# A decoder layer on one core: meta rows folded to 128 partitions, input tiles turned ahead in six PSUM banks, first weight chunk split before them

## The reference

```python
def rmsnorm(x, g):
    xf = x.astype(jnp.float32)
    y = xf * lax.rsqrt(jnp.mean(xf * xf, axis=-1, keepdims=True) + EPS)
    return (y * g.astype(jnp.float32)).astype(x.dtype)
...
    h = jnp.concatenate([meta, x], axis=1)     # (1, 16 + 256, 2048)
    u = rmsnorm(h, pre_mix_g[i])
    proj = u @ w_in[i]                         # 2048 x 4608
    q, k, v, u_pool, u_conv = jnp.split(proj, splits, axis=-1)
    # three head groups, joined and normed, @ w_out, residual
    # u = rmsnorm(h, pre_ffn_g); (silu(u @ w_gate) * (u @ w_up)) @ w_down, residual
```

## Time and profile before

| | us |
|---|---|
| median of 3 runs (lowest, highest) | 1124.66 (1122.86, 1125.36) |
| profiled execution, its own time | 1124.34 |
| its span, first to last instruction | 1122.5 |
| PE busy | 1105.9 |
| DVE busy | 697.9 |
| ACT busy | 528.7 |
| POOL busy | 21.8 |

### The profile page before, as it was taken

How to read it: one execution, slowest core, us unless ns; L and a number is a source line. 1 busy time by engine, 2 the same in 40 slices (tenths; PEclk the granted TensorE clock), 3 DMA queues, 4 the chain that set the end, 5 groups by cost and what they waited for, 6 DMA issues and landing times.

```text
span 1122.5 us, 17667 instructions
## 1 busy us (share of the span) xinstructions
PE 1105.9 (99%) x6544; PEld 979.7 (87%) x6544; DVE 697.9 (62%) x812; ACT 528.7 (47%) x635; POOL 21.8 (2%) x39
## 2 busy tenths in 40 slices
PE   9999999999999999999999999999999999999997
PEld 8999999999888888888888888888888888888885
DVE  5599885646646866666666666666666545444444
ACT  6544444646554564444444444444444434343442
POOL 2000101101000000000000000000000000000000
PEclk9999999999999999999999999999999999999999
DMA  7665534444376366656665666566656555555553
GB/s 245 190 185 168 171 102 125 150 139 135 121 295 211 118 211 213 189 170 201 190 187 177 198 188 189 182 193 191 191 179 195 190 190 197 195 189 197 189 194 111
DMA packets 165998, 203.53 MB, mean 181 GB/s; under 512 B 6304, under 2 KB 133600, under 8 KB 165168
## 3 DMA queue, kind: packets, MB, share of 16 engines
q1 hardware_dynamic: 164800, 197.30, 55.8%
q10 hardware_dynamic: 576, 4.19, 1.0%
q0 software_dynamic: 576, 1.40, 0.4%
HBM read 200.77 MB, written 2.10 MB: 181 GB/s over the span
## 4 chain that ended last, share of the span: by engine, by line
PE 93%; DVE 3%; ACT 2%; DMA 1%; issue 0%; SPq 0%; DVEq 0%; ACTq 0%
PE ps L1065 28%; PE ps L1067 15%; PE ps L1398 7%; PE ps L1397 7%; PE ps L1399 7%; PE ps L1050 5%; PE ps L1052 5%; PE ps L1053 5%; PE ps L1305 3%; PE ps L1307 3%; PE ps L1306 3%; DVE w_lo L724 1%; DMA arena<-in_pre_mix_g 1%; PE ps L1163 1%; PE ps L1249 1%; PE ps L1197 1%
## 5 line engine op out<-in xcount | busy, mean ns | idle before, releaser
L724 DVE TENSOR_TENSOR w_lo<-raw,w_hi 128x1024 fp32r<-128x1024 f32 x368 | 449.4, 1230 | 351.1 <-ACT w_hi L425 350.8
L425 ACT ACTIVATE w_hi<-raw 128x1024 fp32r<-128x1024 f32 x368 | 388.3, 1059 | 474.3 <-PE ps L1067 252.3
L1065 PE MATMUL ps<-u,w_hi 128*128 128x512 f32 x1408 | 491.2, 392 | 1.7 <-DVE u L819 0.8
L1067 PE MATMUL ps<-u,w_lo 128*128 128x256 f32 x1408 | 394.9, 280 | 0.0
L1065 PEld LDWEIGHTS ps<-u,w_hi 128*128 128x128 f32 x1408 | 264.1, 188 | 61.4 <-DVE w_lo L724 1.1
L1067 PEld LDWEIGHTS ps<-u,w_lo 128*128 128x128 f32 x1408 | 265.3, 188 | 0.0
L1050 PE MATMUL ps<-u,w_hi 128*128 128x272 f32 (+1 forms) x576 | 168.9, 293 | 0.0
L1052 PE MATMUL ps<-u,w_hi 128*128 128x272 f32 (+1 forms) x576 | 165.8, 288 | 0.0
L1053 PE MATMUL ps<-u,w_lo 128*128 128x272 f32 (+1 forms) x576 | 165.6, 287 | 0.0
L1399 PE MATMUL ps<-w_hi,ffn 128*128 128x512 f32 x352 | 136.9, 389 | 0.0
L1398 PE MATMUL ps<-w_lo,ffn 128*128 128x512 f32 x352 | 136.9, 389 | 0.0
(11 more groups left out here) (174 smaller groups left out, 625.5 us busy)
## 6 DMA issues: line engine op xcount, KB each, us to landing
raw<-in_w_gate SPq DMA_DIRECT2D x88, 512.0 KB, 4.5
raw<-in_w_up SPq DMA_DIRECT2D x88, 512.0 KB, 4.4
raw<-in_w_down SPq DMA_DIRECT2D x88, 512.0 KB, 4.1
raw<-in_w_in SPq DMA_DIRECT2D x72, 512.0 KB, 3.6
raw<-in_w_out SPq DMA_DIRECT2D x32, 512.0 KB, 4.4
arena<-in_x SPq DMA_DIRECT2D x2, 1024.0 KB, 6.2
arena<-in_x ACTq DMA_DIRECT2D x2, 1024.0 KB, 8.8
out<-f_acc SPq DMA_DIRECT2D x3, 512.0 KB, 2.7
```

What stands on the lines that cost most here:

```text
L425: act.activation(w_hi[:, slot, :], raw[:, slot, :], ACT.Copy).then_inc(hi_done, 1)
L724: dve.tensor_tensor(w_lo[:, slot, :], raw[:, slot, :], hi_view(w_hi[:, slot, :]), ALU.subtract).then_inc(lo_done, 1)
L1065: pe.matmul(ps[:, bank + m, :].rearrange("p (a t) -> p a t", a=2), w_hi[:, slot, at], u[:, kt, :, 0:SEQ], start=first and k == 0, stop=Fal ...
L1067: mm = pe.matmul(ps[:, bank + m, 0:SEQ], w_lo[:, slot, at], u[:, kt, 0, 0:SEQ], start=False, stop=last and k == len(kts) - 1, skip_group_c ...
```

## The change

Meta: its 16 rows of 2048 are loaded as 128 partitions of 256 (partition 8t + s holds eighth s of row t). ACT squares them 256 wide; PE adds the eight partial sums of a row with a matrix of ones in blocks of eight (`blk`, made by POOL with a memset and two selects); ACT scales; PE turns them in two transposes; ACT copies the result (`xmt`), and POOL multiplies by the gain, rounds and subtracts into `u[:, :, :, 0:META]`, before it issues the side weights' DMAs, for which it now also waits for x tile 1. x tiles: DVE squares the first and ACT the second half of each, in the order of their landing; scaled copies come as halves of tile 0 and quarters of tile 1. PE turns them (256 columns per kt) into banks 2 to 7, two kt to a bank (`x_turned`), eighteen transposes before the first product and the others after chunks 0, 1 and 2. The first projection waits for `u_lo` tile by tile (`first_proj`). ACT and DVE split chunk 0 before input tile 0, chunk 1 after tile 5, chunk 2 after tile 9, chunk 3 after tile 13. The gain row is loaded from ACT's queue. The parameter vectors are turned before chunk 4. Fillers: 9, 5 and 19.

```diff
-WARM_LOAD, WARM_ROWS, WARM_PARTS, WARM_FFN = 26, 10, 4, 23
+WARM_LOAD, WARM_SUM, WARM_ROWS, WARM_FFN = 9, 5, 19, 23
...
-    VEC_AT, TURN_AT = 3, 4
+    VEC_AT = CK
+    HALF, QUART = D // 2, D // 4
+    MSEG = P // META
+    XBANKS = 6
...
-            sp_eng.dma_start(xr[0:META, 2, :], meta).then_inc(x_landed[2], 16)
+            sp_eng.dma_start(xr[:, 2, 0:D // MSEG], meta.rearrange("t (s c) -> (t s) c", s=MSEG)).then_inc(x_landed[2], 16)
             for m in range(NQ):
                 sp_eng.dma_start(xr[:, m, :], x[0, m * P:(m + 1) * P, :]).then_inc(x_landed[m], 16)
-            sp_eng.dma_start(grow[0:KT, :], pre_mix_g.rearrange("a (c p) -> (a c) p", p=P)).then_inc(grow_landed, 16)
...
+            pool.memset(blk, 1.0).then_inc(blk_step, 1)
             pool.wait_ge(const_step, 6)
+            pool.wait_ge(blk_step, 1)
+            blk3 = blk.rearrange("p (t s) -> p t s", s=MSEG)
+            pool.affine_select(blk3, blk3, [[-MSEG, META], [0, MSEG]], ALU.is_ge, 0.0, base=0,
+                               channel_multiplier=1).then_inc(blk_step, 1)
+            pool.wait_ge(blk_step, 2)
+            pool.affine_select(blk3, blk3, [[MSEG, META], [0, MSEG]], ALU.is_ge, 0.0, base=MSEG - 1,
+                               channel_multiplier=-1).then_inc(blk_step, 1)
...
+            pool.wait_ge(meta_kept, 1)
+            pool.wait_ge(grow_done, 1)
+            gains = vec[:, V_PRE:V_PRE + KT].rearrange("p (k a) -> p k a", a=1).to_broadcast([P, KT, META])
+            pool.tensor_tensor(xmg, xmt, gains, ALU.mult).then_inc(meta_done, 1)
+            pool.wait_ge(meta_done, 1)
+            pool.tensor_copy(u[:, :, 0, 0:META], xmg).then_inc(meta_done, 1)
+            pool.wait_ge(meta_done, 2)
+            pool.tensor_tensor(u[:, :, 1, 0:META], xmg, u[:, :, 0, 0:META].bitcast(F32), ALU.subtract).then_inc(meta_done, 1)
+            pool.wait_ge(x_landed[1], 16)
             pool.dma_start(wpl, w_pool.rearrange("a g c d -> c (a g) d")).then_inc(sw_landed, 16)
...
+        def x_turned(kt, lo=0, hi=SEQ):
+            at = kt // XBANKS % 2 * SEQ
+            return ps[:, 2 + kt % XBANKS, at + lo:at + hi]
...
+            act.dma_start(grow[0:KT, :], pre_mix_g.rearrange("a (c p) -> (a c) p", p=P)).then_inc(grow_landed, 16)
             act.preload_act_table_set("natural_log_exp_and_others")
             act.wait_ge(const_step, 6)
             act.wait_ge(x_landed[2], 16)
-            act.activation(xsm[0:META], xr[0:META, 2, :], ACT.Square, accum_out=ss0[0:META, 2:3]).then_inc(ss_act, 1)
-            act.wait_ge(ss_act, 1)
-            inv_rms(r0[0:META, 2:3], ss0[0:META, 2:3], D, r0_done)
+            act.activation(xsm, xr[:, 2, 0:D // MSEG], ACT.Square, accum_out=ss0[:, 2:3]).then_inc(ss_act, 1)
+            act.wait_ge(ssm_made, 1)
+            inv_rms(r0[:, 2:3], ps[:, 3, 0:1], D, r0_done)
             act.wait_ge(r0_done, 1)
-            act.activation(xsm[0:META], xr[0:META, 2, :], ACT.Copy, scale=r0[0:META, 2:3]).then_inc(xs_act, 1)
-            act.wait_ge(x_landed[1], 16)
-            act.activation(xs[:, 1, 0:D // 2], xr[:, 1, 0:D // 2], ACT.Square, accum_out=ss0[:, 1:2]).then_inc(ss_act, 1)
-            act.wait_ge(ss_dve, 3)
-            inv_rms(r0[:, 0:2], ss0[:, 0:2], D, r0_done)
-            act.wait_ge(r0_done, 2)
-            act.activation(xs[:, 1, 0:D // 2], xr[:, 1, 0:D // 2], ACT.Copy, scale=r0[:, 1:2]).then_inc(xs_act, 1)
+            act.activation(xsm, xr[:, 2, 0:D // MSEG], ACT.Copy, scale=r0[:, 2:3]).then_inc(xs_act, 1)
             act.wait_ge(grow_turned, 1)
             act.copy(vec[:, 0:KT], ps[:, 0, 0:KT]).then_inc(grow_done, 1)
+            act.wait_ge(meta_turned, 1)
+            act.copy(xmt.rearrange("p (s h) t -> p s h t", h=2),
+                     ps[:, 0, SEQ:2 * SEQ].rearrange("p (h t s) -> p s h t", h=2, s=MSEG)).then_inc(meta_kept, 1)
+            for m in range(NQ):
+                act.wait_ge(x_landed[m], 16)
+                act.activation(xs[:, m, HALF:D], xr[:, m, HALF:D], ACT.Square, accum_out=ssx[:, m, 1:2]).then_inc(ss_act, 1)
+                act.wait_ge(ss_dve, 2 * m + 2)
+                inv_rms(r0[:, m:m + 1], ss0[:, m:m + 1], D, r0_done)
+            def scaled(m, n):
+                cols = slice(n * QUART, (n + 1) * QUART)
+                act.activation(xs[:, m, cols], xr[:, m, cols], ACT.Copy, scale=r0[:, m:m + 1]).then_inc(xs_act, 1)
+            def input_tiles(kts):
+                for kt in kts:
+                    act.wait_ge(u_made, kt + 1)
+                    act.activation(u[:, kt, 0, META:TOK], x_turned(kt), ACT.Copy,
+                                   scale=vec[:, V_PRE + kt:V_PRE + kt + 1]).then_inc(u_hi, 1)
+            split(0)
+            act.wait_ge(r0_done, 3)
+            scaled(1, 1)
             act.wait_ge(grow_done, 1)
-            for kt in range(KT):
-                act.wait_ge(u_made, kt + 1)
-                act.activation(u[:, kt, 0, :], ps[:, 4 + kt % 4, 0:TOK], ACT.Copy,
-                               scale=vec[:, V_PRE + kt:V_PRE + kt + 1]).then_inc(u_hi, 1)
-                if kt % CK == CK - 1:
-                    split(kt // CK)
+            input_tiles(range(0, 6))
+            split(1)
+            input_tiles(range(6, 10))
+            split(2)
+            scaled(1, 3)
+            input_tiles(range(10, 14))
+            split(3)
+            input_tiles(range(14, 16))
...
+            for m in range(NQ):
+                dve.wait_ge(x_landed[m], 16)
+                dve.scalar_tensor_tensor(xs[:, m, 0:HALF], xr[:, m, 0:HALF], 1.0, xr[:, m, 0:HALF], ALU.mult, ALU.mult,
+                                         accum_out=ssx[:, m, 0:1]).then_inc(ss_dve, 1)
+                dve.wait_ge(ss_dve, 2 * m + 1)
+                dve.wait_ge(ss_act, m + 2)
+                dve.tensor_tensor(ss0[:, m:m + 1], ssx[:, m, 0:1], ssx[:, m, 1:2], ALU.add).then_inc(ss_dve, 1)
+            def scaled(m, lo, hi):
+                dve.tensor_scalar(xs[:, m, lo:hi], xr[:, m, lo:hi], r0[:, m:m + 1], None, ALU.mult).then_inc(xs_dve, 1)
+            def input_tiles(kts):
+                for kt in kts:
+                    dve.wait_ge(u_hi, kt + 1)
+                    dve.scalar_tensor_tensor(u[:, kt, 1, META:TOK], x_turned(kt), vec[:, V_PRE + kt:V_PRE + kt + 1],
+                                             hi_view(u[:, kt, 0, META:TOK]), ALU.mult, ALU.subtract).then_inc(u_lo, 1)
             dve.wait_ge(r0_done, 2)
+            scaled(0, 0, HALF)
+            dve.wait_ge(r0_done, 3)
+            scaled(1, 0, QUART)
+            scaled(0, HALF, D)
+            split(0)
+            input_tiles(range(0, 2))
+            scaled(1, HALF, 3 * QUART)
+            input_tiles(range(2, 6))
+            split(1)
+            input_tiles(range(6, 10))
+            split(2)
+            input_tiles(range(10, 14))
+            split(3)
+            input_tiles(range(14, 16))
...
+            pe.wait_ge(blk_step, 3)
+            pe.wait_ge(ss_act, 1)
+            pe.matmul(ps[:, 3, 0:1], blk, ss0[:, 2:3], start=True, stop=True).then_inc(ssm_made, 1)
+            keep_warm(WARM_SUM)
             pe.wait_ge(const_ready, 1)
             pe.wait_ge(grow_landed, 16)
             pe.transpose(ps[:, 0, 0:KT], grow[0:KT, :], ident[0:KT, 0:KT]).then_inc(grow_turned, 1)
+            pe.wait_ge(xs_act, 1)
+            pe.wait_ge(grow_done, 1)
+            for h in range(2):
+                mm = pe.transpose(ps[:, 0, SEQ + h * P:SEQ + (h + 1) * P], xsm[:, h * P:(h + 1) * P], ident)
+            mm.then_inc(meta_turned, 1)
             keep_warm(WARM_ROWS)
+            def turn_rows(m, kts):
                 for kt in kts:
+                    if m == 0:
+                        pe.wait_ge(xs_dve, 1 if kt < KT // 2 else 3)
+                        if kt >= 2 * XBANKS:
+                            pe.wait_ge(u_lo, kt - XBANKS + 1)
+                    else:
+                        if kt < CK:
+                            pe.wait_ge(xs_dve, 2)
+                        elif kt < KT // 2:
+                            pe.wait_ge(xs_act, 2)
+                        elif kt < 3 * CK:
+                            pe.wait_ge(xs_dve, 4)
+                        else:
+                            pe.wait_ge(xs_act, 3)
+                        if kt >= XBANKS:
+                            pe.wait_ge(u_lo, kt - XBANKS + 1)
+                    mm = pe.transpose(x_turned(kt, m * P, (m + 1) * P), xs[:, m, kt * P:(kt + 1) * P], ident)
+                    if m == 1:
+                        mm.then_inc(u_made, 1)
+            pe.wait_ge(r0_done, 1)
+            turn_rows(0, range(0, 8))
+            turn_rows(1, range(0, 2))
+            turn_rows(0, range(8, 12))
+            turn_rows(1, range(2, 6))
+            pe.wait_ge(meta_kept, 1)
+            pe.wait_ge(meta_done, 3)
+            LATER = {0: [(1, range(6, 10))], 1: [(1, range(10, 12)), (0, range(12, 14)), (1, range(12, 14))],
+                     2: [(0, range(14, 16)), (1, range(14, 16))]}
...
```

(17 more changed lines are left out.)

47 lines of the change are left out of this document (10 added, 37 removed).

## The result

The changed kernel takes 1118.19 us (median of 5 runs, 1117.63 to 1118.53) beside 1124.66 (1122.86 to 1126.67); the ratio is 0.9941, 95% interval 0.9927 to 0.9956: 6.5 us faster (5.0 to 8.2 by the interval), where 5.1 were forecast.

The account below looks back on a forecast made before the run. TensorE, busy 99% of the span, was taken as the bound. Gain 5.1 us: 3.55 before the first product, 4.06 of turns replaced by 1.54, less 1.0 new waiting; 1124.66 - 5.1 = 1119.56, rounded 1119.5, range 1117.0 to 1122.4.

Parts of the forecast that it names:

- The sum: Whole kernel: fifth chunk starts at 30.0 instead of 35.10 us, so the time falls by 5.1 us.
- The block: Everything after the fifth chunk's start moves as one: what the fifth chunk gains, the end gains.
- the late fall: Granted clock drops in mid kernel after L1197's longest wait, costing about 1.6 us; it may vanish or double.
- Rival (c): L1197's waits, 60 to 100 us: VectorE work at absolute times gives the gain back, time 1124.5; chance 0.05.
- Part 1: PE's own work: turns at 0.11 us each between the first chunks, 1.54 us replacing 4.06.
- Part 2: Chain from meta rows and x scales to the first product: 14.75 us, 3.55 earlier than before.
- Rival (b): ScalarE's start chain is 0.75 us shorter (1118.8) or up to 1.8 longer (1121.4); chance 0.2.
- Part 3: Chunks 0 to 3, following ACT and DVE in order: fifth chunk at 30.0 us, with 1.0 of new waiting.
- split 1 to 17.6: ACT's order at the start: six input tiles 13.7 to 16.55, then the split of chunk 1 until 17.6 us.
- the waits for VectorE's w_lo: Expected sign in the new profile: PE's waits at the start are for VectorE's low weight parts, not for POOL.
- Rival (a): Before the first product: if turns count as idle, TensorE's clock falls, costing 1.6 us, time 1121.1; chance 0.3.
- rival (d): Start: PE waits for POOL's meta tile, with POOL steps of 4.7 us instead of 1.6, time 1127; chance 0.03.

Follow-up runs that it names:

- after_again: The changed kernel itself, unaltered, measured once more in a later series: median 1118.17 us, fifth chunk at 29.65 us.
- late_fill: The changed kernel with nine filler products in front of PE's wait for the second head pair's weights, near 162 us: median 1117.53 us.
- late_split: The changed kernel with chunk 0 split after input tiles 0 to 3, as before, not ahead of them: median 1121.25 us.
- fillers_as_turns: The changed kernel with the 19 filler products before the x turns replaced by 38 transposes of the identity: 1117.78 us (one run).
- no_row_fillers: The changed kernel without the 19 filler products before the x turns, so that PE idles there: 1120.20 us (one run).
- short_chain: The changed kernel with 6, 3, 22 fillers, VectorE splitting chunk 0 earlier, four early turns moved behind chunk 0: median 1119.86 us.

## Why the prediction held, step by step

- **The sum.** 5.1 us were forecast; 6.5 and 6.1 came in the medians of two series, 6.4 and 5.4 in the two traces (fifth chunk 28.61 and 29.65). The mechanism came as forecast, and the gain was forecast too small. In the first trace all errors have one sign and add up to 1.4 us, below; in after_again a later first product takes half of them back, and that its 5.4 is so near is luck.
- **The block.** The assumption held to 0.1 us between the profiled executions, and under a forced delay once the late fall is taken off. Rival (c), a backlog of DVE at absolute times, is out.
- **Part 1, turns.** 0.11 us each, as taken from the earlier trace rows. With what stands around them (the gap to the next product) the three gaps are 0.34, 0.68 and 0.38 us, 1.40 together, for 1.54 in the sum and 4.06 before. The vector turns: 28.61 - 25.16 - 3.10 = 0.35, as before.
- **Part 2, the chain.** 14.46 for 14.75. PE reached the sum at 4.77, not 5.1, and the meta copy began at 7.23 and left ACT at 7.50 for 7.85. Meta landed at 3.04 (expected 3.67), the gain row in time. Rival (b) had its range right, but on the late side not for its reasons: the pace at which the first fillers run changes somewhere between 4.4 and 7.5 us, at another time in each execution, and x tile 1 lands between 8.97 and 10.23. In after_again PE came to the sum at 5.21, ACT squared x tile 1 from 10.23 in place of 9.39, and with the same program the first product came at 15.48 and the fifth chunk 1.04 later. With late_fill, the same up to there, at 15.56, the first product lies between 14.5 and 15.6, and my 14.75 was near the early end.
- **Part 3 failed in one term.** "Input tiles each 0.48", "split 1 to 17.6": I took the duration of an ACT instruction for its start-to-start time. Six tiles took 2.30 us in flight, so (2.30 - 0.47) / 5 = 0.37 each; four splits in a row 3.90, so 0.95 each for a duration of 1.06. Before, the tiles stood 0.53 apart because PE turned them at that pace, and the durations gave no sign of it. On six tiles and two splits that is 0.9 us, about the waiting of 0.65 + 0.3 us ahead of chunks 1 and 3 that I put in and that isn't there: the waits for VectorE's w_lo, which I had named as a sign, don't appear in the trace. With the 0.3 of part 2 and 0.14 of the turns it makes the 1.4 us between 30.0 and 28.61; in after_again part 2 is 0.73 late instead, and 0.35 is left. For DVE's scaled copies I had used the start-to-start time (0.67), and it held: 1.90 us from the first of the three (10.72) to the split (12.62), for 1.8. The Trainium skill (ScalarE: Activation LUTs, section What ACT_TABLE_LOAD costs) gives the overlap of back-to-back ACTIVATEs as about 93 ns; this case's trace has 0.10 to 0.11.
- **Rival (a), the clock.** It didn't occur in the changed kernel, but its price and place were right for late_split. Its reason was wrong: the clock stayed up through turns (fillers_as_turns) and fell where they were left out and PE idled (no_row_fillers). The Trainium skill (TensorE: Matmul & The Clock Gate, section PE-mode transpose) says that a transpose doesn't count as PE being busy; fillers_as_turns doesn't agree, with 6.6 us of turns in a stretch of 7.4 at 1.00.
- **POOL, rival (d).** POOL's three steps ended at 10.78, PE asked for them at 13.9. Two-input steps of 128x256 cost 0.63 us, not 1.6:

```profile
7.80 0.63 POOL L401 TENSOR_TENSOR side<-side,cst 128x256 f32<-128x256 f32 x1
...
8.97 1.81 POOL L405 TENSOR_TENSOR u<-side,u 128x256 fp32r<-128x256 f32 x1
```

The step at 8.97 took 1.81 us as it began together with DVE's square (8.97 to 10.20) and ended 0.58 behind it. In late_split (first two rows) POOL was first, and in short_chain (last row) DVE's add met POOL's first step (7.80 to 8.99):

```profile
9.34 0.73 POOL L405 TENSOR_TENSOR u<-side,u 128x256 fp32r<-128x256 f32 x1
...
9.49 1.66 DVE L782 SCALAR_TENSOR_TENSOR xs<-arena 128x1024 f32<-128x1024 f32 x1
...
8.55 0.46 DVE L785 TENSOR_TENSOR cst<-cst 128x1 f32<-128x1 f32 x1
```

The square took 1.66 us in place of 1.23, the add 0.46 in place of 0.16. So each is held up by the other, whoever is first, as the prediction had it as a bound. The loss fell on POOL in the changed kernel, where there was room; in late_split at most 0.15 us of it reached the chain, in short_chain nothing, since x tile 1 landed later still.
